# Moving small input transfers and one prefetch behind or ahead of weight units at the head of a two-block transformer kernel

## The reference

```python
mod = jax.nn.silu(c) @ w_mod[l] + b_mod[l]                    # c: 1 x 1024, w_mod: 1024 x 6144
sh_m, sc_m, gt_m, sh_f, sc_f, gt_f = jnp.split(mod, 6)        # shift, scale and gate, twice
h = rms_norm(x, g_mix_norm[l]) * (1.0 + sc_m) + sh_m
proj = h @ w_in[l]                                            # q_a k_a v_a q_i k_i w_i q_b k_b v_b gate_a gate_b
q_i = apply_rope(q_i, cos_i, sin_i)                           # 8 heads of 64
q_b = apply_rope(rms_norm(q_b, g_q_moba[l]), cos_h, sin_h)    # 4 heads of 128; k_b, q_a, k_a alike
...
x = x + gt_m * (merged @ w_out[l])
```

## Time and profile before

| | |
|---|---|
| three timed executions | 1488.47, 1491.34, 1492.21 us (median 1491.34) |
| profiled execution | 1494.77 us, of which the span of the trace is 1492.7 us |
| PE busy | 1450.2 us, 97% of the span |
| DVE, ACT busy | 849.1 us (57%), 689.3 us (46%) |
| moved by DMA | 271 MB, mean 182 GB/s |

### The profile page before, as it was taken

How to read it: one execution, slowest core, us unless ns; L and a number is a source line. 1 busy time by engine, 2 the same in 40 slices (tenths; PEclk the granted TensorE clock), 3 DMA queues, 4 the chain that set the end, 5 groups by cost and what they waited for, 6 DMA issues and landing times.

```text
span 1492.7 us, 17981 instructions
## 1 busy us (share of the span) xinstructions
PE 1450.2 (97%) x6910; PEld 1161.4 (78%) x6910; DVE 849.1 (57%) x1033; ACT 689.3 (46%) x880; POOL 36.1 (2%) x53
## 2 busy tenths in 40 slices
PE   6999999999999999999999999999999998999998
PEld 3757777788888888888888888788888865788887
DVE  2687766554556545466755455565445658655444
ACT  2454454444344444454454444754444667554442
POOL 0010100000000000000000000200000020000000
PEclk9999999999999999999999999999999989999999
DMA  9763767455564655546555655555555510455551
GB/s 343 272 224 113 244 222 264 133 196 187 179 196 156 211 179 187 194 157 200 182 177 189 188 179 196 148 191 178 195 184 183 191 41 29 141 178 189 190 190 70
DMA packets 188163, 271.13 MB, mean 182 GB/s; under 512 B 8380, under 2 KB 134148, under 8 KB 188100
## 3 DMA queue, kind: packets, MB, share of 16 engines
q1 hardware_dynamic: 186448, 267.01, 54.3%
q10 hardware_dynamic: 1492, 2.98, 0.7%
q0 software_dynamic: 160, 0.26, 0.2%
HBM read 269.19 MB, written 1.05 MB: 181 GB/s over the span
## 4 chain that ended last, share of the span: by engine, by line
PE 84%; DVE 6%; ACT 3%; DMA 3%; issue 2%; SPq 1%; POOL 0%; ACTq 0%; DVEq 0%
PE bank L1821 25%; PE bank L1823 25%; PE bank L1822 25%; DVE w_lo_ring L1327 2%; PE bank L1851 2%; DMA raw_ring<-in_w_mod_dram 1%; ACT w_hi_ring L982 1%; PE bank L1991 1%; DMA raw_ring<-in_w_in_dram 1%; PE bank L2123 1%; PE bank L2045 1%; PE bank L2144 1%; SPq L885 1%; PE bank L1879 0%; PE bank L1959 0%
## 5 line engine op out<-in xcount | busy, mean ns | idle before, releaser
L1327 DVE TENSOR_TENSOR w_lo_ring<-raw_ring,w_hi_ring 128x2048 fp32r<-128x2048 f32 (+1 forms) x226 | 513.8, 2277 | 401.6 <-ACT w_hi_ring L1270 329.8
L1821 PE MATMUL bank<-w_hi_ring,h_hi 128*128 128x512 f32 x1360 | 543.5, 400 | 2.2 <-DVE h_lo L1475 1.0
L1823 PE MATMUL bank<-w_hi_ring,h_lo 128*128 128x512 f32 x1360 | 531.8, 391 | 0.0
L1822 PE MATMUL bank<-w_lo_ring,h_hi 128*128 128x512 f32 x1360 | 530.9, 390 | 0.0
L1270 ACT ACTIVATE w_hi_ring<-raw_ring 128x2048 fp32r<-128x2048 f32 x158 | 302.8, 1917 | 295.8 <-PE bank L1823 292.5
L1821 PEld LDWEIGHTS bank<-w_hi_ring,h_hi 128*128 128x128 f32 x1360 | 256.2, 188 | 66.5 <-issue 15.6
L1823 PEld LDWEIGHTS bank<-w_hi_ring,h_lo 128*128 128x128 f32 x1360 | 255.8, 188 | 54.9
L1822 PEld LDWEIGHTS bank<-w_lo_ring,h_hi 128*128 128x128 f32 x1360 | 256.4, 189 | 49.4
L1821 PE MATMUL bank<-w_hi_ring,f_hi 128*128 128x512 f32 (+1 forms) x456 | 177.1, 388 | 0.0
L1823 PE MATMUL bank<-w_hi_ring,f_lo 128*128 128x512 f32 (+1 forms) x456 | 176.0, 386 | 0.0
L1822 PE MATMUL bank<-w_lo_ring,f_hi 128*128 128x512 f32 (+1 forms) x456 | 175.7, 385 | 0.0
(11 more groups left out here) (259 smaller groups left out, 873.1 us busy)
## 6 DMA issues: line engine op xcount, KB each, us to landing
raw_ring<-in_ffn_w_gate_up_dram SPq DMA_DIRECT2D x176, 512.0 KB
raw_ring<-in_ffn_w_down_dram SPq DMA_DIRECT2D x44, 1024.0 KB
raw_ring<-in_w_in_dram SPq DMA_DIRECT2D x22, 1024.0 KB
raw_ring<-in_w_gate_up_dram SPq DMA_DIRECT2D x44, 512.0 KB
arena<-in_w_mod_dram SPq DMA_DIRECT2D x18, 1024.0 KB, 7.1
raw_ring<-in_w_down_dram SPq DMA_DIRECT2D x11, 1024.0 KB
raw_ring<-in_conv_w_in_dram SPq DMA_DIRECT2D x16, 512.0 KB
raw_ring<-in_w_mod_dram SPq DMA_DIRECT2D x6, 1024.0 KB
```

The source lines that it names most:

```text
L1327: dve.tensor_tensor(w_lo[:, u % RING, 0:words], raw[:, r % RING, 0:words], w_hi[:, u % RING, 0:words].bitcast(F32), ALU.subtract).then_inc ...
L1821: pe.matmul(dst, hi, whi, start=start, stop=False)
L1822: pe.matmul(dst, hi, wlo, start=False, stop=False)
L1823: return pe.matmul(dst, lo, whi, start=False, stop=stop)
```

## The change

The tables leave ACT's queue, where they stood behind the gains after `xh` 1, and are issued by SP right behind qi's part 1. The gains and the gate's bias are issued by ACT after `xh` 3: the gains stood after `xh` 1, the bias behind ACT's copy of ki. Both halves of mod 4 are put into the list ahead of qi's part 1; its second half stood behind ki. The warm products go from ten to six.

```diff
-    part("qi", 0, 0, 2, [mod_sum(1), [dict(kind="warm", times=10)], mod_a[1:], [dict(kind="then split", unit=1 - RING)], xh[2:]],
+    part("qi", 0, 0, 2, [mod_sum(1), [dict(kind="warm", times=6)], mod_a[1:], [dict(kind="then split", unit=1 - RING)], xh[2:]],
          [mod_sum(3) + mod_row(1, 0), mod_row(1, 1)])
-    part("qi", 0, 1, 2, [evac("qi"), mod(4, 0)])
-    part("ki", 0, 0, 1, [mod_row(4, 0), evac("ki"), mod(4, 1)])
+    plan.extend(mod_load(4))
+    part("qi", 0, 1, 2, [evac("qi")])
+    part("ki", 0, 0, 1, [mod_row(4, 0), evac("ki")])
...
                 fill(r % RING, words, src)
+                if raws[r] == ("unit", find["unit", "qi", 0]):
+                    sp.dma_start(const[:, C_COSH:], A["const"][:, C_COSH:]).then_inc(sem("tables_full"), 16)
...
-                if k == "xh" and g == 1:
+                if k == "xh" and g == 3:
+                    act.wait_ge(sem("t_done"), find["tg", "mrow", (0, 3)] + 1)
+                    act.dma_start(gt[:, 0, :], A["b_mod"][0:1, 2 * D:3 * D].to_broadcast([P, D])).then_inc(sem("gt_full0"), 16)
                     for i, g in enumerate(("g_q_dsa", "g_k_dsa", "g_q_moba", "g_k_moba")):
                         act.dma_start(gains[:, i, :], A[g].to_broadcast([P, HD])).then_inc(sem("gains_full"), 16)
-                    act.dma_start(const[:, C_COSH:], A["const"][:, C_COSH:]).then_inc(sem("tables_full"), 16)
...
                         act.activation(kiw_t[0:72, :], b[0][0:72, 0:T], ACT.Copy).then_inc(free, 1)
-                        act.dma_start(gt[:, 0, :], A["b_mod"][0:1, 2 * D:3 * D].to_broadcast([P, D])).then_inc(sem("gt_full0"), 16)
```

## The result

| | before | after |
|---|---|---|
| median of 11 runs each, same session | 1488.94 us | 1495.85 us |
| ratio | | 1.0035, 95% interval 1.0024 to 1.0046 |
| a later session (35 and 12 runs) | 1490.05 us | 1493.84 us |
| ratio | | 1.0019, 95% interval 1.0006 to 1.0032 |
| profiled execution: time, span | 1494.77, 1492.7 us | 1498.37, 1496.4 us |

The ratio and its interval are worked out from the single runs; they are not the quotient of the two medians (1.0046 and 1.0025).

The account below looks back on a forecast made before the run. PE was taken as the bound, busy 97% of the span. A gain of 3.25 us at `kiu` plus 0.4 at the gate's sum made -3.6 us: 1487.7 us against the median of 1491.34 (-0.24%), range 1485.7 to 1490.6.

Parts of the forecast that it names:

- the start of qi's second part: PE's products on qi's part 1: start at 42.9 us instead of 46.28, 3.4 earlier (2.7 to 4.4).
- `kiu` at 55.5: PE's transpose of ki: at 55.5 us (54.4 to 56.1 at PE, 53.8 to 57.1 by the landing), gaining 3.25.
- the step of the warm products: PE ahead of qi's second part: six products take at most 5.0 us, 38.1 to 43.1; ten had ended at 46.3.
- the landing of qb's part 1: SP's queue: this transfer lands at 52.5 us (50.8 to 54.1), delayed by the moved transfers.
- The base of 48.9: SP's queue: qb's part 1 would land at 48.9 us in the new order without ACT's bias and gains.
- The term of bias and gains: Delay of SP's queue: bias 1.3 to 1.8 us, gains 0.64 to 3.4, together 1.9 to 5.2, taken as 3.6.
- `kiu` follows the landing: ACT's split of qb's part 1, two copies and handovers: PE can transpose ki 3.0 us after the landing.
- slower rival: Bias and gains stall SP's dense queue; no gain from a landing at 55.75 us on; up to 1494.9 us; chance 0.05.
- qi's part 1 landed: SP's queue: with gains and tables gone, qi's part 1 lands at 32.6 us; ACT had waited for it until 38.50.
- the rival that the place has no effect: qi's part 1 still lands at 38.5 us; only fewer warm products gain, 2.0 us, giving 1489.3; chance 0.05.
- Mod 1's second half: SP's queue: it lands at 30.0 us, so PE starts it 0.71 us earlier, at 35.15.
- The 0.4 us at the gate's sum: DVE's wait to take up mod 4's sum, held by the low part of kb's part 1, goes: 0.4 us gained.

Follow-up runs that it names:

- e5: The changed kernel run and profiled again in a later session, nothing edited; ratio to the kernel before 1.0019.
- e8: The kernel before the change run and profiled again, nothing edited; ratio 1.0001.
- e12: The kernel before the change with only both halves of mod 4 fetched ahead of qi's second part; ratio to the kernel before 0.9997.
- e10: The kernel before the change with six warm products instead of ten, nothing else; ratio to the kernel before 1.0001.
- e2: The changed kernel with the four gains issued behind ACT's copy of ki instead of after `xh` 3; ratio to the kernel before 1.0010.
- e9: The changed kernel with the bias alone back behind ACT's copy of ki; ratio to the kernel before 1.0004.
- e6: The changed kernel with bias and gains issued by ACT right behind its split of qi's part 1; ratio to the kernel before 0.9999.
- e3: The changed kernel with nine products on constants ahead of `kiu`, for PE to run while it waits; ratio to the kernel before 1.0011.
- e4: The changed kernel with ten warm products again instead of six; ratio to the kernel before 1.0009.
- e1: The changed kernel with mod 4's halves back in their old place, behind qi and ki; ratio to the kernel before 1.0007.

## Why the prediction was wrong

**The first failed step is the start of qi's second part, "3.4 us earlier than 46.28".** The value that I forecast (42.9) was nearly met, 43.82 and 43.08. In part that is luck: `mod_s` came at 40.40 and 39.67, not at 38.5 to 39.0, and no product behind it ran at half speed. The value that I took it from was not the kernel's: 46.28 came from ten warm products at a clock of 0.50, which is one execution's. Counted from PE's start of mod 1's second half, so that executions can be compared, qi's second part starts 6.80 us later in after and e5. In the kernel before it was 10.42 us in the execution that I had and 7.07 in e8; in e12, whose edit touches only transfers behind it, 8.00. So with the clock up the change has 0.3 to 1.2 us to gain here, not 3.4; and `kiu` at 55.5, as forecast, is where e8 has it with nothing changed (55.66). I had the sign in my rows: the profiled execution was 3.4 us above the median, and I put the sum against the median without asking where those 3.4 us lay. Against e8 it is 6.5 us longer, and 3.1 of these are there at the start of mod 5 (71.86 against 68.72), in the stretch that I was costing; the rest came later. e10 shows the step of the warm products right at that clock (2.2 us) and worth nothing over its runs.

**The second is the landing of qb's part 1, 52.5 (50.8 to 54.1).** It was 57.42 and 56.46. The base of 48.9 was right (49.38 in e12). The term of bias and gains, 3.6 us in 1.9 to 5.2, was too small: 56.46 - 49.38 = 7.1 us. One at a time beside e12 they are 2.1 for the bias (e2, 51.51) and 4.6 for the gains (e9, 53.97), together 6.7. These profiles do not all start the stretch at the same time, though: qb's part 0 landed at 41.67 in e12, 42.10 in e2, 42.43 in e9, 42.30 in e5 and 44.05 in after. Counted from there, the bias costs 1.7, the gains 3.8, and both 6.5 in e5 and 5.7 in after. I had 1.3 to 1.8 and 0.64 to 3.4, and took the middle because a full queue "may or may not suffer". It suffered more than the half-empty one. DMA in 40 to 58 us, in 40 slices (busy tenths, then GB/s), of the changed kernel again:

```profile
DMA  9999999999999999499987969999999999999999
GB/s 423 405 400 405 396 419 414 419 410 423 396 409 297 224 240 184 125 217 234 228 141 133 141 148 340 365 409 411 419 405 437 387 373 400 396 401 391 396 401 400
...
q10 hardware_dynamic: 720, 0.79, 18.6%
...
arena<-in_g_k_moba_dram ACTq DMA_DIRECT2D x1, 64.0 KB, 11.2
```

and of the kernel before with mod 4 ahead:

```profile
GB/s 414 401 401 400 423 414 400 405 414 414 405 400 419 401 414 405 400 423 410 405 400 396 378 391 391 96 36 0 0 0 0 73 77 223 264 300 269 373 355 351
```

The engines are busy for 4 to 9 tenths of each slice, but from 45.4 to 50.8 us (12 slices of 0.45 us) they move a mean of 193 GB/s instead of 410. That loses 1.17 MB or 2.9 us. The transfers' own bytes are 1.9 us. The last of the 16 completions of qb's part 1 came 1.4 us after the one before it (55.04 and 56.46), in e12 0.04 us. And qb's part 0 was 0.6 us later from the start. Together 6.8 of the 7.1 us. The Trainium skill ("DMA: Bandwidth & Descriptors", section "Issuing engines are not separate DMA queues") says that transfers of several engines interleave on the same 16; by that alone it would have been, as an estimate, the 1.9 us. The trace agrees that they share (the rate falls while both queues move), and has 4 to 5 us more. Why it falls is not shown by these runs.

**From the landing on, the steps held, and led to a loss.** `kiu` follows the landing by 2.82 to 2.83 us in after, e5, e6 and e9 (I had 3.0). PE gets there at about 55.6 where the clock is up, so the point from which the landing costs is 55.6 - 2.8 = 52.8, not 55.75 as my slower rival had it. That rival was right in kind: the broadcast reads stall the queue in the middle of a dense stretch, at 1.6 to 2 times my middle price. I gave it 0.05, for the point of no gain had 3 us of one execution's low clock in it.

**What I had not thought of is the clock behind the wait.** It fell at 58 to 59 us in both profiles of the changed kernel, after PE's waits of 3.70 and 3.91 us. Of the extra time some 2.2 us are not the clock, by an estimate: taking half of the low-clock time off the spans leaves a mean of 1480.0 to 1480.1 us in the two sessions, and 1477.8 for the kernel before. The rest, 1.7 to 2.9 us, is 3.4 to 5.8 us more at half speed. This split is worked out from rounded means, uncertain by up to 1 us. e3 fits it: its time at the low level is that of the kernel before, and 1479.9 us are left. The Trainium skill ("TensorE: Matmul & The Clock Gate", section "What's actually happening") says that the throttled clock is the default and that activity releases it; I judged that by qi's products alone, and did not apply it to a wait of PE further on. The rows of 56 to 60 us agree with it. In e4 the clock stayed up through a shorter wait of 3.12 us; what decides between the two is open.

**What held.** qi's part 1 landed at 34.16 and 33.75, 3.6 to 4.3 us earlier (I had 32.6), so the gains and the tables were what delayed it, and the rival that the place has no effect falls. Whether qi's second part waits for it differs from execution to execution. In e8 it does not: ACT's split ends at 39.33 and DVE takes the low part at 39.42, directly behind `mod_s`. In e12 it does, DVE first and then PE:

```profile
40.09 2.29 DVE L1328 TENSOR_TENSOR w_lo_ring<-raw_ring,w_hi_ring 128x2048 fp32r<-128x2048 f32 x1 [1.11 <-ACT w_hi_ring L983]
...
43.59 0.47 PE L1822 MATMUL bank<-w_hi_ring,h_hi 128*128 128x512 f32 x1 [0.58 <-DVE h_lo L1438]
```

Mod 1's second half did not move forward (37.02 and 36.28, against 36.11 in e8), since PE itself reaches it no earlier there; a wait for it as in the earlier trace rows stands in one more profile, e10 (1.06 us), and in neither e8 nor e12. The 0.4 us at the gate's sum came: DVE's step follows PE's at once, and PE's wait there went to 0.35 us from 0.73 in the kernel before:

```profile
70.52 0.66 PE L1997 MATMUL bank<-const,arena 128*128 128x128 f32 x4 [0.73 <-DVE arena L1463]
```

## What to carry to other kernels

Before a gain is summed from one profile, look at the granted clock of the very stretch: a start that stands behind warm-up products at the low clock may be that execution's; a second profile, or the mean clock of the other runs, helps to tell whether the kernel has it. When transfers leave a stretch where they delay one unit, follow the queue to the unit that will be late in the other stretch, and price broadcast reads there by no less than the worst row at hand; here four reads of 64 KB cost a full queue 3.8 to 4.6 us, where the worst row had 3.4. An engine that takes its work in order hands such a delay on: ki's copy, long possible, stood behind a split that had no data.

## What the runs showed of the hardware

Four broadcast reads of 64 KB and one of 512 KB, 0.79 MB in all, delayed a full queue by 5.7 to 7.1 us, where their bytes at 410 GB/s are 1.9.

The last of a unit's 16 completions can come late, unit after unit: in e5 by 1.42, 1.42 and 1.28 us behind the one before it at qb's part 1, kb's part 0 and part 1; in e8 by 0.05, 0.27 and 0.11. At qb's part 1 it was 1.3 to 1.5 us in after, e3, e4 and e5, but 0.19 in e1, where the same reads stand ahead of it, and 1.09 at e5's qi part 1, ahead of which no such read was issued. So the reads are not shown to be the cause, nor that it is the same DMA engine each time, which the trace does not name.

The clock's second fall at 38.0 to 38.5 us was there in the three profiles whose first low stretch ran from 21.0-21.5 to 27.8-28.3, and in none of the other eleven. What shifts the first stretch from execution to execution is not known from these runs.
